# Forgetting-attention scores as two one-pass products of high and low parts, with the gate sums in the second product's free rows

## The reference

```python
def forgetting_attention(q, k, v, f_logit):
    qh = q.astype(f32).transpose(0, 2, 1, 3) * (d ** -0.5)
    c = jnp.cumsum(jax.nn.log_sigmoid(f_logit.astype(f32)), axis=1).transpose(0, 2, 1)
...
        s = jnp.einsum('bhqd,bhkd->bhqk', qb, kh) + cb[..., :, None] - c[:, :, None, :]
        s = jnp.where(kpos[None, :] <= qpos[:, None], s, -jnp.inf)
        return jnp.einsum('bhqk,bhkd->bhqd', jax.nn.softmax(s, axis=-1), vh)
```

## Time and profile before

| | |
|---|---|
| median of 3 runs | 4439.3 us (4424.22 to 4443.81) |
| profiled execution | 4428.86 us, its span 4427.1 us |
| PE busy | 4278.4 us (97% of the span) |
| DVE, POOL, ACT busy | 3092.1, 2817.6, 1800.0 us |
| four attention rounds, first layer | 245.2 to 449.1 us of the span |
| four attention rounds, second layer | 2446.1 to 2650.5 us |

### The profile page before, as it was taken

The page is one execution under the profiler, slowest core; times in us unless marked ns, Lnnn a source line. Parts: engine busy times, 40 slices in busy tenths (PEclk is TensorE's granted clock), DMA queues, the critical chain, the costliest instruction groups (busy, mean ns, idle before and its releaser), DMA issues.

```text
span 4427.1 us, 74587 instructions
## 1 busy us (share of the span) xinstructions
PE 4278.4 (97%) x21290; PEld 3665.3 (83%) x21290; DVE 3092.1 (70%) x5263; ACT 1800.0 (41%) x3318; POOL 2817.6 (64%) x1633
## 2 busy tenths in 40 slices
PE   8999999999999999999999999999999999999998
PEld 6777876779999998788777778767899999978887
DVE  6666435647788667898866664366487887678988
ACT  4145123124576663333331550231245766533333
POOL 6843764765577666676668438647655776756665
PEclk9999999999999999999999999999999999999999
DMA  3233844734599999999822339448246999989997
GB/s 108 91 105 105 261 149 137 230 99 138 198 352 348 314 302 308 346 354 348 294 82 90 110 96 290 133 133 245 78 143 208 350 359 305 316 300 346 351 349 273
DMA packets 494913, 1011.86 MB, mean 229 GB/s; under 512 B 51536, under 2 KB 320464, under 8 KB 491856
## 3 DMA queue, kind: packets, MB, share of 16 engines
q1 hardware_dynamic: 420656, 739.77, 51.7%
q0 software_dynamic: 73728, 268.47, 17.0%
q10 hardware_dynamic: 288, 1.05, 0.1%
HBM read 846.57 MB, written 162.53 MB: 228 GB/s over the span
## 4 chain that ended last, share of the span: by engine, by line
PE 84%; DMA 4%; DVE 3%; ACT 3%; issue 3%; POOL 2%; SPq 1%; DVEq 0%; ACTq 0%; POOLq 0%
PE bank L1367 13%; PE bank L1424 7%; PE bank L1419 7%; PE pair L1020 7%; PE bank L1429 7%; PE bank L1371 6%; PE bank L1020 6%; PE pair L1022 4%; PE bank L1398 3%; PE bank L1046 3%; PE bank L1022 3%; PE pair L1046 2%; PE bank L1087 2%; PE pair L1087 2%; DMA ring<-u_tab 2%
## 5 line engine op out<-in xcount | busy, mean ns | idle before, releaser
L873 POOL TENSOR_TENSOR w_hi<-ring,ones 128x1024 fp32r<-128x1024 f32 x272 | 540.6, 1988 | 702.4 <-PE bank L1046 238.8
L1367 PE MATMUL bank<-xT,w_hi 128*128 128x384 f32 x2048 | 710.1, 347 | 5.4 <-ACT w_hi L1846 3.4
L876 POOL TENSOR_TENSOR w_lo<-ring,w_hi 128x1024 fp32r<-128x1024 f32 x272 | 692.9, 2548 | 21.4
L1367 PE MATMUL bank<-xl_peer,w_hi 128*128 128x384 f32 x2048 | 689.5, 337 | 0.0
L860 POOL TENSOR_TENSOR w_lo<-ring,w_hi 128x1024 fp32r<-128x1024 f32 x192 | 462.9, 2412 | 306.8 <-ACT w_hi L1846 305.8
L867 POOL TENSOR_TENSOR cl<-att,ch 128x384 fp32r<-128x384 f32 x256 | 376.5, 1471 | 327.4 <-ACT ch L1921 315.5
L1852 ACT CAST w_hi<-ring 128x1024 fp32r<-128x1024 f32 x252 | 265.4, 1053 | 665.8 <-PE bank L1429 465.3
L2724 DVE TENSOR_TENSOR w_lo<-ring,w_hi 128x1024 fp32r<-128x1024 f32 x252 | 342.2, 1358 | 121.5 <-ACT w_hi L1852 119.7
L1419 PE MATMUL bank<-w_hi,ch 128*128 128x512 f32 x1524 | 389.4, 391 | 12.6 <-ACT ch L1921 12.6
L1371 PE MATMUL bank<-xT,w_lo 128*128 128x384 f32 x2048 | 396.9, 334 | 0.0
L1367 PEld LDWEIGHTS bank<-xT,w_hi 128*128 128x128 f32 x2048 | 388.7, 190 | 6.8 <-issue 3.8
(11 more groups left out here) (404 smaller groups left out, 9416.1 us busy)
## 6 DMA issues: line engine op xcount, KB each, us to landing
ring<-v_tab SPq DMA_DIRECT2D x252, 512.0 KB, 7.0
ring<-w_stream SPq DMA_DIRECT2D x240, 512.0 KB, 3.8
g_spill<-gst SPq DMA_DIRECT2D x240, 192.0 KB, 4.6
vg<-w_spill SPq DMA_DIRECT2D x64, 704.0 KB, 10.2
att<-u_tab SPq DMA_DIRECT2D x320, 128.0 KB, 4.6
u_turned<-att SPq DMA_DIRECT2D x80, 512.0 KB, 5.6
ring<-u_tab SPq DMA_DIRECT2D x256, 128.0 KB, 3.6
ring<-u_turned SPq DMA_DIRECT2D x64, 512.0 KB, 5.6
```

The source lines that it names most:

```text
L873: nc.gpsimd.tensor_tensor(w_hi[b][:, 0:n], src, ones[:, 0:1].to_broadcast([P, n]), ALU.mult)\
L876: nc.gpsimd.tensor_tensor(w_lo[b][:, 0:n], src, w_hi[b][:, 0:n].bitcast(F32), ALU.subtract)\
L1367: nc.tensor.matmul(out, w_hi[s % 2][:, c * P:(c + 1) * P], dense_parts(c)[part], start=(c == 0 and part == 0), stop=False)
```

## The change

S becomes two one-pass products that add up in the same bank. The first multiplies the high part of the keys, which stands in both halves of the 128 rows, with the high part of the head's queries in its own half and their low part in the other. The second multiplies the low part of the keys in the head's own half with the high part of the queries; in its other half, which the head doesn't need, stand the parts of all gate sums with a minus, against a 0/1 column that picks the head (`of_head`). So `C`, `sel`, `cb` and the subtraction go, and the score tile of each head is a tile of its own, no longer two tiles in turn by rounds.

The scores stay in PSUM: DVE adds the mask in place, takes the maximum from there, and ACT's exponential reads the bank and gives it back. So `S u` now waits for the exponential of unit `u - 2`, where it waited for DVE's subtraction.

ACT makes the high parts, for each head one instruction of 64x1024 and one of 64x512 for the queries, two of 64x512 for the keys (`fox_query_high`, `fox_key_high`); DVE makes the low parts (`fox_low`, 64x512, two a slot). For the first pair of heads of the next round this is done behind units 5 and 7, for the second pair behind units 0 and 2 of the round itself, in the fourth round behind S 1 and S 2. The first round's parts are made from a float32 copy (`fox_raw`) in five pieces (`fox_first_pair`, `fox_first_lows`), three ahead of the round; the third waits for the end of `MA`.

```diff
 def fox_steps():
-    seq = [("C", 0)]
+    seq = []
     for k in range(16 + 3):
         if k < 16:
             seq.append(("S", k))
-        if k % 4 == 2 and k < 13:
-            seq.append(("C", k // 4 + 1))
         if 2 <= k < 18:
             seq.append(("T", k - 2))
...
                             fill_wait(b, L, "FQ", i, u // 2)
-                            nc.tensor.matmul(bank[b][:, 0:(t + 1) * P], fox_q[i % 2][pp][hp][:, t * P:(t + 1) * P],
-                                             fox_k[i % 2][pp][:, 0:(t + 1) * P], start=True, stop=True)\
-                                .then_inc(filled[b].sem, 1)
+                            for a in range(2):
+                                mm = nc.tensor.matmul(bank[b][:, 0:(t + 1) * P], fox_q[pp][hp][:, a, t * P:(t + 1) * P],
+                                                      fox_k[pp][hp][:, a, 0:(t + 1) * P], start=(a == 0), stop=(a == 1))
+                            mm.then_inc(filled[b].sem, 1)
                         elif kind == "T":
-                            pe.wait_ge(prob_ready.sem, prob_ready.at(L, "FQ", i, u + 1))
+                            fill_wait(b, L, "FQ", i, u // 2 + 1)
...
+                def fox_query_high(i, pp, hp, src, scale):
+                    own, other = slice(64 * hp, 64 * hp + 64), slice(64 - 64 * hp, 128 - 64 * hp)
+                    h = 4 * i + 2 * pp + hp
+                    nc.scalar.activation(fox_q[pp][hp][own, :, :], src[own, :].unsqueeze(1).to_broadcast([64, 2, SEQ]),
+                                         ACT.Copy, scale=scale)
+                    return nc.scalar.copy(fox_q[pp][hp][other, 1, :], of_head[other, h:h + 1].to_broadcast([64, SEQ]))
+
+                def fox_key_high(pp, hp, src):
+                    own, other = slice(64 * hp, 64 * hp + 64), slice(64 - 64 * hp, 128 - 64 * hp)
+                    nc.scalar.copy(fox_k[pp][hp][own, 0, :], src[own, :])
+                    return nc.scalar.copy(fox_k[pp][hp][other, 0, :], src[own, :])
+
+                def fox_sums(pp, hp):
+                    for part in range(2):
+                        at = 64 - 64 * hp + 32 * part
+                        ins = nc.scalar.activation(fox_k[pp][hp][at:at + 32, 1, :], row_parts[0:32, part, :].bitcast(F32),
+                                                   ACT.Copy, scale=-1.0)
+                    return ins
...
+                    elif n == 2:
+                        act.wait_ge(proj_done, slots_done(L, "MA", 3, 4))
+                        stand(act)
+                        fox_sums(0, 1)
+                        ins = fox_key_high(0, 1, fox_raw[1])
...
-                            nc.scalar.activation(pr[:, e % 2, 0:ne], sc[:, e % 2, 0:ne], ACT.Exp,
+                            nc.scalar.activation(pr[:, e % 2, 0:ne], bank[4 + e % 2][:, 0:ne], ACT.Exp,
                                                  bias=nmax[:, e:e + 1], accum_out=rsum[:, e:e + 1])\
-                                .then_inc(prob_ready.sem, 1)
+                                .then_inc(drained_sem[4 + e % 2], 1)
...
+                        if i == 0 and kind == "V" and u in (0, 2):
+                            fox_first_pair(3 + u // 2)
+                        if 0 < i < 3 and kind == "V" and u in (0, 2):
+                            fox_query_key(i, 2 + u // 2)
+                        if i == 3 and kind == "S" and u in (1, 2):
+                            fox_query_key(i, 1 + u)
...
+                        if kind == "V" and u in (5, 7) and i < 3:
...
+                            fox_query_key(i + 1, (u - 5) // 2)
...
+                fox_first_lows(0)
+                fox_first_lows(1)
                 merge_round(L, "MA", 3)
+                fox_first_lows(2)
...
-                            V.tensor_tensor(sc[:, u % 2, 0:n], bank[b][:, 0:n], cb[:, h % 2, 0:n], ALU.subtract)\
-                                .then_inc(drained_sem[b], 1)
-                            dve.wait_ge(drained_sem[b], drained[b].at(L, "FQ", i, u // 2 + 1))
-                            diag = sc[:, u % 2, n - P:n]
+                            diag = bank[b][:, n - P:n]
                             c.step(V.tensor_tensor(diag, diag, mask_q[:, :], ALU.add))
```

More of the change, by code:

```diff
@@ L1153, in _ @@
                                              ident[0:ML_H, 0:ML_H])
-                mm.then_inc(filled[7].sem, 1)
+                    if t % 2:
+                        mm.then_inc(filled[7].sem, 1)
                 for i in range(4):
@@ L1165, in _ @@
                         b = 4 + u % 2
[L1166 to L1172, removed]
-                        elif kind == "S":
-                            pp, hp = h // 2, h % 2
-                            if u in (0, 8):
+                        if kind == "S":
+                            pp, hp = h // 2, h % 2
+                            if i == 0 and t == 0:
+                                pe.wait_ge(fox_first_low.sem, fox_first_low.at(L, "FQ", 0, (1, 2, 4, 4)[h]))
+                                if h == 3:
+                                    pe.wait_ge(fox_sums_ready.sem, fox_sums_ready.at(L, "FQ", 0, 1))
+                            elif u in (0, 8):
                                 for s in (2 * pp, 2 * pp + 1):
@@ L1639, in _ @@
                 merge_gates(L, "MA", 0, 1)
-                act.wait_ge(filled[7].sem, filled[7].at(L, "COLS", 0, 1))
-                nc.scalar.copy(gcol[:, :, :], bank[7][:, 0:TT * ML_H].rearrange("p (t n) -> p t n", t=TT))\
-                    .then_inc(drained_sem[7], 1)
+                for n in range(3):
+                    fox_first_pair(n)
+                act.wait_ge(filled[7].sem, filled[7].at(L, "COLS", 0, 2))
+                for z in range(2):
+                    nc.scalar.copy(gcol[:, 2 * z:2 * z + 2, :],
+                                   bank[7][:, 2 * z * ML_H:(2 * z + 2) * ML_H].rearrange("p (t n) -> p t n", t=2))\
+                        .then_inc(drained_sem[7], 1)
                 for i in range(4):
-                    n7 = beside = 0
+                    n7 = 0
                     todo = []
-                    for (kind, u), dense in zip(fox_steps(), fox_beside()):
+                    for kind, u in fox_steps():
                         t, h = u % 4, u // 4
@@ L2232, in _, with fox_low @@
                     pass
+                def fox_low(s, hp, src, scale):
+                    pp = s // 2
+                    own, other = slice(64 * hp, 64 * hp + 64), slice(64 - 64 * hp, 128 - 64 * hp)
+                    if s % 2:
+                        to, hi = fox_k[pp][hp][own, 1, :], fox_k[pp][hp][own, 0, :]
+                    else:
+                        to, hi = fox_q[pp][hp][other, 0, :], fox_q[pp][hp][own, 0, :]
+                    return V.scalar_tensor_tensor(out=to, in0=src[own, :], scalar=scale, in1=hi.bitcast(F32),
+                                                  op0=ALU.mult, op1=ALU.subtract)
@@ new lines, in fox_first_lows, with fox_low_part @@
+                def fox_first_lows(n):
+                    dve.wait_ge(fox_first_high.sem, fox_first_high.at(L, "FQ", 0, n + 1))
+                    s, heads = ((0, (0, 1)), (1, (0,)), (1, (1,)), (2, (0, 1)), (3, (0, 1)))[n]
+                    for hp in heads:
+                        ins = fox_low(s, hp, fox_raw[s], 1.0)
+                    if n:
+                        ins.then_inc(fox_first_low.sem, 1)
+                def fox_low_part(i, s):
+                    dve.wait_ge(fox_high[s // 2].sem, fox_high[s // 2].at(L, "FQ", i - 1, s % 2 + 1))
+                    fox_low(s, 0, bank[s], 1.0 if s % 2 else FOX_D ** -0.5)
+                    fox_low(s, 1, bank[s], 1.0 if s % 2 else FOX_D ** -0.5).then_inc(drained_sem[s], 1)
@@ L2264, in scores_and_roots @@
+                        if u in (9, 11) and not last:
+                            fox_low_part(i + 1, (u - 9) // 2)
                         if u % 4 == 3 and (u > 3 and not last or u == 3 and not first):
```

133 lines of the change are left out of this document (74 added, 59 removed).

## The result

The changed kernel took 4444.2 us (median of 20 runs, 4432.6 to 4454.9) against 4431.8 for the kernel before beside it: ratio 1.003, 95% interval 1.0022 to 1.0037. It is 12 us slower: a small difference, within the 0.5% that the forecast called no change, but clear of the noise. The profiled execution has a span of 4440.6 us, 13.5 more than before.

A forecast was written before the change was run, and what follows sets the result against it. PE was taken as the bound. Per layer -21.3 (PE's work) + 6.6 (round starts) + 4 (clock) + 9.3 (inside rounds) = -1.4, -2.8 in both; against the median 4439.3 that gave 4436 us, range 4405 to 4464.

The forecast's parts named there:

- PE's saving goes into its own waits: Likeliest case, over the attention rounds: PE's saved work returns as PE waits, time within 0.5% of no change; chance 0.62.
- PE's work: Attention rounds: cheaper S products and no spreads of the gate sums save PE 21.3 us a layer.
- the lower bound of -22.9: PE's work a layer if one-pass product time goes by columns down to 128; the other bound was -11.7.
- The spread: Gate sums spread by two one-pass products of 512 columns, 0.47 us; dropping four saves 1.9 us a round.
- Rival (4): S products below 512 columns take 0.235 us each: PE gains 11.7, about 4450 us, still within 0.5%; chance 0.10.
- Where a round begins: S 2 waits for the chain mask, maximum, exponential: PE idles 14.4 us against 7.8, +6.6 a layer.
- the dearer end: First round's S 2: if POOL's w_lo starts before DVE's low part, PE idles 4.8 us; otherwise 2.4.
- Inside the round: ACT's in-order pieces delay copies PE needs at later steps of each round: +9.3 us a layer (2 to 25).
- The walk: ACT's order traced step by step: waits at T 3 and around ACT's pieces, 2.3 us a round.
- The 1.4 of the fourth round: Two pieces behind S 1 and S 2, 4.9 us ahead of T 0's copy: 1.4 us wait beyond the start's idle.
- rival (3): Slower by ACT: its 64-row or spread-column instructions cost more than their columns; +18 a layer, 4475 us; chance 0.11.
- The clock: Longer idles at the four round starts lower the granted clock: +4 us a layer (0 to 5).

The follow-up runs named there:

- e1_turn: Changed kernel with DVE's turn of an expert tile moved from ahead of the mask to behind the same unit's maximum: 4436.5 us, 1.0009 to the kernel before.
- e7_narrow: Changed kernel with ACT's pieces of rounds 2 to 4 writing 16 of 512 columns, so most scores use stale columns: ratio 0.9933 to the kernel before.
- e4_last: Changed kernel with the fourth round's keys on ACT moved from behind S 2 to behind V 0, their low part to unit 4: 4447.2 us, 1.0029.
- b1_moved: Kernel before the change, with y_lo moved behind the maximum of unit 1 and DVE's turns behind the maxima: 4426.4 us, 0.9987.
- e8_order: Changed kernel with e5_both's moves and ACT's pieces by heads, reordered where e6_spread waited, low parts following each head: 4401.4 us, 0.993 to the kernel before.
- e6_spread: Changed kernel with e5_both's moves and ACT's pieces spread by heads, one a step: 4415.9 us, ratio 0.996 to the kernel before.
- e5_both: Changed kernel with the moves of e1_turn and e3_start together: 4424.1 us, ratio 0.9982 to the kernel before.
- e9_fill: Changed kernel with eight more one-pass products of 512 columns ahead of S 2 in each round: 4435.2 us, ratio 1.0003 to the kernel before.
- e3_start: Changed kernel with masks 0 and 1 ahead of y_lo, and the first round's third piece and its low part behind unit 1: 4430.3 us, 0.9998.
- e2_split: Changed kernel with ACT's next-round queries split by heads, one behind V 5, the other behind V 6: 4466.9 us, 1.0079 to the kernel before.

## Why the prediction was right and wrong

The forecast was 4436 us, 3 under the base of 4439.3, and "PE's saving goes into its own waits". That mechanism is what happened, and the time lies in the range, but the direction was missed: the kernel is 12 us slower than the kernel before. That 4436 and 4444 lie so near is in part luck. The base, a median of 3 runs, was 7 us above that of 20, and of the terms two missed by 3 us a layer to the good and two by 4 and 6 to the bad. Term by term, a layer:

- **PE's work**, forecast -21.3, was **-24.4**, past the lower bound of -22.9. The products came as worked out: four undisturbed steps, S 11 to S 15, took 10.24 us against 11.08 before, 0.84 a head where 0.86 was said. The spread was priced too low. From S 10 to S 11 in the fourth round, before and then after:

```profile
425.10 0.81 PE L1180 MATMUL bank<-qk 128*128 128x384 f32 x2
...
429.52 1.02 PE L1180 MATMUL bank<-qk 128*128 128x512 f32 x2
```
```profile
430.63 0.51 PE L1175 MATMUL bank<-fox_k,fox_q 128*128 128x384 f32 x2
...
433.85 0.71 PE L1175 MATMUL bank<-fox_k,fox_q 128*128 128x512 f32 x2
```

  4.42 against 3.22, so 1.20 where 0.29 for S and 0.47 for the spread were counted. Start to start missed what the spread cost behind it: V 7, which needs bank 7 emptied of the spread by ACT, began 0.49 us after the product ahead of it (427.02 to 427.51; ACT's copy ended at 427.46), now 0.24, a stop too short to stand in the list of waits. Over the stage the four spreads of a round come to 2.7 us (24.4 / 4 less 3.4 for S), 0.7 each. Rival (4) is out.
- **Where a round begins**, forecast +6.6, was **+3.6**: S 2 idles 4.3, 2.3, 2.4, 2.4 where 3.6, 2.7, 5.2, 2.9 were said. In the first round the low part came behind POOL's `w_lo`, as the dearer end had it. In the third `y_lo` came first this time, and POOL's `w_lo` took 3.30 us instead of 2.36. The Trainium skill's page "SBUF — State Buffer" (SBUF: two separate sides) has the lock for whoever starts first; the trace agrees in both orders, 2.36 us for DVE's 0.69 behind POOL in the first pair of rows and 3.30 for POOL behind DVE in the second:

```profile
246.24 2.34 POOL L885 TENSOR_TENSOR w_lo<-ring,w_hi 128x1024 fp32r<-128x1024 f32 x1
246.77 2.36 DVE L2301 SCALAR_TENSOR_TENSOR fox_k<-att,fox_k 64x512 fp32r<-64x512 f32 x1 [1.96 <-ACT fox_k L1576]
```
```profile
351.26 1.22 DVE L2120 TENSOR_TENSOR y_lo<-big,y_hi  x1 [3.29 <-ACT y_hi L1723]
351.42 3.30 POOL L885 TENSOR_TENSOR w_lo<-ring,w_hi 128x1024 fp32r<-128x1024 f32 x1
```

- **Inside the round**, forecast +9.3, was **+16.3 and +15.2**: this is the step that failed. By rounds the first layer waits 4.5, 3.9, 3.9 and 4.1 us, where 3.3, 2.3, 2.3 and 1.4 were said. The walk's waits at T 3 (2.41 in the first round against 2.1, 1.14 in the next two against 1.1) and for the keys behind V 7 (1.1 in the first round against 0.8) held. "0.3 for the queries behind V 5" was 2.73 in two rounds. The prediction put DVE at nothing ("it ends each before the next S, so nothing"), and so the walk left out DVE's turn and its transfer, which make the exponential late just where the long piece stands behind it; `e1_turn` and `e7_narrow` show that it takes both. The 1.4 of the fourth round was 4.05 (2.48 in the second layer): the two pieces took 5.7 us, not 4.9, and the copy of T 0 stands behind all of it; with the keys moved away (`e4_last`) T 1 waited 0.2. The pieces were too short in the sum as well. By shape, over the stage (count, busy us, mean ns, idle us ahead):

```profile
L1570 ACT CAST fox_q<-of_head 64x512 fp32r<-64x512 f32 x14 | 8.6, 615 | 0.2
L1568 ACT ACTIVATE fox_q<-bank 64x1024 fp32r<-64x1024 f32 x6 | 6.1, 1014 | 0.0
L1576 ACT CAST fox_k<-bank 64x512 fp32r<-64x512 f32 x6 | 3.5, 580 | 0.1
```

  Each is priced by its columns, as said, which rules out rival (3). But the 0.1 us of overlap that was taken off each did not come between the pieces of rounds 2 to 4: the rows under `e1_turn` start 1.02, 0.63 and 1.03 us apart. That makes 3.3 us instead of 2.9 and 2.35 instead of 2.0.
- **The clock**, forecast +4, was **+7.7** in the stage. Over the 20 runs the mean granted clock was 0.987, against 0.993 in the runs of the kernel before: 26 us more lost in the whole program, twice the slowdown. By the profiles 15 of them lie in the two stages; where the others come from stays open. The forecast counted the starts of the rounds and "1 off" for later waits. The waits inside the rounds brought spells of their own, 3.4 us of lost clock from T 1 of the fourth round alone (410.5 to 417.5).

What the profile was to show came for S 2, for the products, for T 3 and for ACT's shapes. "No wait longer than that later in a round" did not, and the low clock stood behind two of the four starts in the first layer and three in the second, not behind all.

## What to carry to other kernels

When work moves from the bound engine to engines with room, the busy share (ACT 130 of 208 us) doesn't tell the price: walk each new piece through its engine's order, together with every wait that already stands there, the ones that cost nothing so far too. Here pieces of 3 us in an order whose steps take 2.5 us made waits; with the turn and the start of the rounds mended the waits of a layer went from 27 us to 19, and with the same load cut into pieces of about 1.5 us, one a step and clear of the copies PE needs next, to 11. A follower (here DVE's low part) has to move with the piece that it waits for.

## What the runs showed of the hardware

The clock does not follow the length of one wait. The same 2.4 us ahead of T 3 of the first round brought no lower clock in the changed kernel and a spell of 6.8 us at the lower level in `e1_turn` and in `e4_last`; in `e7_narrow` it brought none in the first layer and one in the second. The same 1.81 us ahead of `MV` brought none before, and in the changed kernel one behind the first layer (0.59 from 455 to 459) and none behind the second. In the stages of all kernels each spell cost about 1.7 us or twice that, and their sum rose with the sum of the waits, with much scatter. No run changes the clock and leaves the waits, so this shows that the two go together, not how. Each figure is from one execution; waits are without those ahead of `MV`:

| kernel | waits, us (first, second layer) | clock lost, us |
|---|---|---|
| `b1_moved` | 4.1, 4.1 | 0, 0 |
| before | 7.9, 7.9 | 1.7, 1.7 |
| `e8_order` | 10.8, 10.9 | 1.7, 1.7 |
| `e7_narrow` | 14.1, 14.1 | 5.1, 10.2 |
| `e6_spread` | 18.6, 18.9 | 5.1, 1.7 |
| `e5_both` | 19.4, 19.4 | 5.1, 5.1 |
| `e9_fill` | 20.1, 19.9 | 8.6, 8.5 |
| `e3_start` | 21.5, 21.0 | 10.2, 11.9 |
| `e1_turn` | 25.1, 25.2 | 10.2, 10.2 |
| changed kernel | 27.7, 26.6 | 10.2, 8.6 |
| `e4_last` | 28.5, 27.0 | 15.4, 15.4 |
| `e2_split` | 32.6, 31.9 | 20.5, 22.2 |
